# Half of a branch slab moved into a recurrent mixer's state scan, and gate products between its groups of small products

## The reference, cut to what matters

```python
# third branch: the recurrence, here in chunks of 64 positions
def step(state, inp):
    r_t, w_t, k_t, v_t, kk_t, a_t = inp
    sa = jnp.einsum("bhvk,bhk->bhv", state, kk_t)
    state = (state * w_t[:, :, None, :]
             - sa[..., None] * (kk_t * a_t)[:, :, None, :]
             + v_t[..., None] * k_t[:, :, None, :])
    return state, jnp.einsum("bhvk,bhk->bhv", state, r_t)
...
gates = jax.nn.sigmoid(proj[..., OFF_GATE:OFF_RWKV].reshape(b, s, N_BRANCH, D_MODEL) + gate_b)
branches = jnp.einsum("bsnc,ncd->bsnd", ys, branch_proj)   # ys: conv, attention, recurrence
merged = jnp.einsum("bsnd,bsnd->bsd", gates, branches)
return merged @ w_mix_out, v_first
```

## Time and profile before

| what | us |
|---|---|
| median of 3 runs | 1669.34 |
| lowest and highest run | 1667.26, 1671.3 |
| the profiled execution, in all | 1670.32 |
| its span, first to last instruction | 1667.9 |

### The profile page before, as it was taken

The page is one execution under the profiler, slowest core; times in us unless marked ns, Lnnn a source line. Parts: engine busy times, 40 slices in busy tenths (PEclk is TensorE's granted clock), DMA queues, the critical chain, the costliest instruction groups (busy, mean ns, idle before and its releaser), DMA issues.

```text
span 1667.9 us, 29552 instructions
## 1 busy us (share of the span) xinstructions
PE 1633.1 (98%) x12590; PEld 1497.5 (90%) x12590; DVE 1239.9 (74%) x1358; ACT 922.4 (55%) x1015; POOL 37.5 (2%) x40
## 2 busy tenths in 40 slices
PE   8999999999999999999999999999999999999997
PEld 7988998999999998888999988888888897988887
DVE  6677877975788888776697787657876678677655
ACT  5376534544566557554576655448555456555445
POOL 0000000100000000000020000000000000000000
PEclk9999999999999999999999999999999998999999
DMA  8524445453454544555633455553555541445551
GB/s 295 185 90 169 160 143 202 153 206 122 158 197 181 201 161 167 202 195 187 212 133 127 165 212 188 181 198 130 201 199 189 169 177 72 167 179 184 189 187 54
DMA packets 84136, 287.14 MB, mean 172 GB/s; under 512 B 5856, under 2 KB 54112, under 8 KB 56384
## 3 DMA queue, kind: packets, MB, share of 16 engines
q1 hardware_dynamic: 79984, 273.70, 46.6%
q0 software_dynamic: 2816, 10.69, 1.8%
q10 hardware_dynamic: 1232, 1.25, 0.2%
HBM read 281.42 MB, written 4.19 MB: 171 GB/s over the span
## 4 chain that ended last, share of the span: by engine, by line
PE 86%; DVE 7%; ACT 3%; issue 1%; DMA 1%; POOL 0%; ACTq 0%; DVEq 0%; POOLq 0%
PE PS L476 86%; DVE arena L2151 2%; DVE ring_lo L2148 2%; ACT arena L1484 1%; DVE arena L2148 1%; ACT ring_hi L1484 1%; DMA arena<-spilled_gates 1%; DMA residual<-in_x_t 0%; ACT L1484 0%; ACT operand L1484 0%; DVE arena L2308 0%; DMA ring_raw<-in_w_stream 0%; DVE inv L2207 0%; DVE residual L2148 0%; PE PS L922 0%
## 5 line engine op out<-in xcount | busy, mean ns | idle before, releaser
L476 PE MATMUL PS<-operand,ring_hi 128*128 128x256 f32 (+1 forms) x4360 | 905.6, 329 | 12.7 <-DVE operand L2213 10.2
L476 PEld LDWEIGHTS PS<-operand,ring_hi 128*128 128x128 f32 x4360 | 727.6, 191 | 80.3 <-DVE ring_lo L2148 8.1
L2148 DVE TENSOR_TENSOR ring_lo<-ring_raw,ring_hi 128x2048 fp32r<-128x2048 f32 (+2 forms) x267 | 601.8, 2257 | 203.6 <-ACT ring_hi L1484 203.1
L1484 ACT ACTIVATE ring_hi<-ring_raw 128x2048 fp32r<-128x2048 f32 (+2 forms) x267 | 497.2, 1863 | 192.3 <-PE PS L476 184.7
L476 PE MATMUL PS<-operand,ring_lo 128*128 128x256 f32 x3060 | 601.9, 283 | 0.1
L476 PEld LDWEIGHTS PS<-operand,ring_lo 128*128 128x128 f32 x3060 | 479.9, 192 | 12.0 <-DVE ring_lo L2148 0.4
L1484 ACT ACTIVATE arena<-PS 128x512 f32<-128x512 f32 (+2 forms) x141 | 89.7, 642 | 175.9 <-PE PS L476 164.0
L476 PE MATMUL PS<-hidden,ring_hi 128*128 128x512 f32 x704 | 174.8, 396 | 0.0
L476 PEld LDWEIGHTS PS<-hidden,ring_hi 128*128 128x128 f32 x704 | 128.0, 188 | 26.2
L2148 DVE TENSOR_TENSOR arena<-arena,PS 128x512 f32<-128x512 f32 (+4 forms) x147 | 99.6, 683 | 28.0 <-ACT arena L1484 21.6
L1484 ACT ACTIVATE arena<-arena 128x512 f32<-128x512 f32 (+6 forms) x124 | 85.4, 702 | 59.8 <-DVE arena L2151 32.8
(11 more groups left out here) (160 smaller groups left out, 1125.0 us busy)
## 6 DMA issues: line engine op xcount, KB each, us to landing
ring_raw<-in_w_stream SPq DMA_DIRECT2D x215, 1024.0 KB, 4.8
ring_raw<-in_w_stream SPq DMA_DIRECT2D x64, 512.0 KB, 4.4
ring_raw<-in_w_stream SPq DMA_DIRECT2D x52, 256.0 KB, 3.5
spilled_gates<-arena POOLq DMA_DIRECT2D x12, 256.0 KB, 2.7
arena<-spilled_gates POOLq DMA_DIRECT2D x2, 1536.0 KB, 9.8
tables<-in_tables POOLq DMA_DIRECT2D x1, 1344.0 KB, 9.7
residual<-in_x_t ACTq DMA_DIRECT2D x4, 256.0 KB, 7.7
arena<-in_mem_t POOLq DMA_DIRECT2D x1, 1024.0 KB, 16.6
```

What stands on the lines that cost most here:

```text
L476: return nc.tensor.matmul(out, lhs, rhs, start=start, stop=stop, skip_group_check=True)
L1484: return nc.scalar.activation(out, in_, func, **kw)
L2148: return v.tensor_tensor(out, a, b, op)
```

## The change

- gate_half takes a range of tiles, so that a half can be issued in two pieces.
- gate_slab(4), which stood ahead of the second pairs, is issued as one half ahead of them and one behind. On VectorE the masking of these pairs goes ahead of take_gates(4).
- In the levels, the first three tiles (9 MATMULs) of the second gate half stand between add_to_yt and add_to_y, the other five behind add_to_y.
- Output tiles 2 and 3 of branch slab 0 (24 of its 48 MATMULs, bank 7) are issued in the scan, in three pieces: 9 behind added and carrier, 9 ahead of propagated(2), 6 between carried(2) and carried(3). The waits for the operand and for the slab's low part move ahead of the first piece. Tiles 0 and 1 stay behind the scan.
- So that bank 7 is free, added(1) goes to the second half of bank 2, added(0) and added(2) to the halves of bank 6.
- ScalarE's copy of the transitions waits for the second rk_update in place of a signal of its own.
- VectorE's split of the slab gates + 14 (the third branch slab) goes behind rk_out.

The number of products and of instructions on VectorE and ScalarE stays as it is.

```diff
-            def gate_half(n, m):
+            def gate_half(n, m, ks=range(KT)):
...
-                for k in range(KT):
+                for k in ks:
                     last_ = block_product(out, slot, m * KT + k, XH[:, k, :], XL[:, k, :], k == 0, k == KT - 1)
-                if m == 1:
+                if m == 1 and k == KT - 1:
...
-            gate_slab(4)
+            gate_half(4, 0)
             pe.wait_ge(sem("rk_masked"), 1)
             token_pairs(4, K_, KK).then_inc(sem("rk_pairs"), 1)
+            gate_half(4, 1)
...
                     last.then_inc(sem("rk_dyt"), 1)
+                gate_half(5 + li, 1, range(0, 3))
                 for j in range(8):
...
                 last.then_inc(sem("rk_dy"), 1)
-                gate_half(5 + li, 1)
+                gate_half(5 + li, 1, range(3, KT))
...
-                o = bank(6 + c)[rows_of(q), tt * 4 * HD + f * HD:tt * 4 * HD + (f + 1) * HD]
+                first = (0, 4, 4)[gc] * HD + f * HD
+                o = bank(2 if c else 6)[rows_of(q), first:first + HD]
...
+            operands(2)
+            pe.wait_ge(lo_split, place(START["branch"])[2] + 1)
+
+            def branch_products(m, ks):
+
+                for k in ks:
+                    last_ = block_product(tiles_of(6, 4)[:, m, :], place(START["branch"])[0], 4 * m + k, XH[:, 8 + k],
+                                          XL[:, 8 + k], k == 0, k == 3)
+                return last_
...
-            low.then_inc(sem("rk_transition"), 1)
             up.then_inc(sem("rk_update"), 1)
+            branch_products(2, range(0, 3))
...
-            pe.wait_ge(sem("rk_transition"), 2)
+            pe.wait_ge(sem("rk_transition"), 1)
...
+            branch_products(2, (3,))
+            branch_products(3, range(0, 2))
             pe.wait_ge(sem("rk_state"), 2)
             propagated(2)
...
             carried(2).then_inc(sem("rk_carried"), 1)
+            branch_products(3, range(2, 4))
...
-            operands(2)
-            branch_slab(0, 6)
+            branch_products(0, range(4))
+            branch_products(1, range(4)).then_inc(multiplied, 1)
...
-            act.wait_ge(sem("rk_transition"), 1)
+            act.wait_ge(sem("rk_update"), 2)
...
-            take_gates(4)
             dve.wait_ge(sem("rk_pairs"), 2)
             masked_results(Fm, 4, "before", "rk_masked")
+            take_gates(4)
...
-                step(tt_(new, new, chunk_part(7) if gc == 1 else chunk_part(6, 1), ALU.add))
+                step(tt_(new, new, chunk_part(2 if gc == 1 else 6, 1), ALU.add))
...
             next_state(2)
-            split_slab(START["gates"] + 14)
             dve.wait_ge(sem("rk_inner_copied"), 1)
...
             last.then_inc(sem("rk_out"), 1)
+            split_slab(START["gates"] + 14)
             output_gains()
```

## The result

The changed kernel takes 1675.3 us (median of 7 runs, 1672.1 to 1676.7) against 1669.3: ratio 1.0032, 95% interval 1.0023 to 1.0041, so 5.3 us slower, outside the range of the prediction and above its bound for a change. The profiled execution took 1672.1 us, its span is 1670.1; it is the fastest of the seven, so its trace shows less of the loss than the median does.

What follows compares the result with a forecast made beforehand. Bound after the scan: VectorE's rk_out, the gates' reload, then VectorE's fixed chain to 307.57, not TensorE's end of slab 0. The terms put the gates 1.0 us later, so 1669.3 + 1.0 = 1670.3 us, range 1666.5 to 1673.0.

Steps and rivals of the forecast that it cites:

- The reload: Gates' reload after rk_out: the slab issued in its way costs between 0 and 2.7 us; gates land at 281.6, 1.0 later.
- TensorE's head start on slab 0: After the scan: TensorE some 1.45 us ahead on branch slab 0, then idle about 3 us before branch slab 4.
- the rule of turns between queues: In the reload: DMA engines alternate queues packet by packet, so the slab's whole 2.7 us is paid: 282.5, 1671.2 at the end.
- rival 1: Reload goes in order of request, memory operand off the path; only rk_out counts: -0.8, 1668.5 us; chance 0.20.
- rk_out: VectorE's signal behind the scan comes at 266.4, 0.8 us earlier; the scan's last small product ends at 265.4.
- Up to the scan: Gate slab 4 and the levels together: 0.3 + 1.4 - 1.44 - 0.7 = -0.45 us.
- The stalls near 188 and 200: TensorE's late instruction blocks at 189.38 and 200.35: the change wins 1.44 us at the first, 0.7 at the second.
- the cuts: In levels 1 to 4, a run of 128 small products is cut in two: 4 x 0.35 = 1.4 us lost.
- the gate slab's part: Gate slab 4 split round the second pairs: one more switch, +0.3 us; stall near 188 gone, -1.44.
- The levels' part: Nine gate products between Yt's and Y's groups: +1.4 us for cut runs, -0.7 for covering the stall at 200.35.
- Rival 3: Block behind gate slab 5 still late: 1.44 us not won, the second stall's 0.7 falls too; 1672.4 us; chance 0.15.
- rival 2: Scan stalls are waits that inserted products fill; VectorE's chain has slack: -2.3, 1667.0 us, at best 1664.0; chance 0.13.

Runs made afterwards that it cites:

- second profiles: One more execution of each kernel, unchanged: the kernel before, 1666.7 us, and the changed kernel, 1675.0 us.
- b1: The kernel before with only the split of slab gates + 14 moved behind rk_out: 1672.4 us, ratio 1.0019.
- b4: The kernel before with only the 24 branch products in the scan, with their banks and ScalarE's wait; split in its old place: 1673.5 us, ratio 1.0023.
- a3: The changed kernel with the split of slab gates + 14 back in its old place, ahead of the additions: 1673.9 us, ratio 1.0028 to the kernel before.
- a1: The changed kernel with SP holding the load of weight slab branch + 5 until the gates have landed: 1669.3 us, 1.0000 of the kernel before.
- c1: The kernel before with the split of slab gates + 14 behind rk_out and the load it releases held until the gates have landed: 1669.2 us, ratio 0.9992.
- d0: The changed kernel once more, unchanged, for a second profile: 1675.0 us, one execution.

## Why the prediction was wrong

The forecast was 1670.3 with no change that can be measured; it is 1675.3. The step that failed is the price of the slab in the reload's way, taken at 1.8 us and measured at 3.8 to 4.2. The frame held: the chain over rk_out, the reload and VectorE's fixed 27 us is what sets the end, and TensorE's head start on slab 0 was spent on standing still (3.3 us of idleness before slab 4, predicted about 3). Three terms in the frame were off, all to the same side, the reload's by the most.

**The reload (+1.8 taken, +3.8 in the shown pair, +4.2 by the second profiles).** The prediction had both ends, 0 and 2.7, and took a value between them. The slab's issue came at 269.97, 2.5 us behind rk_out as predicted (268.9 said, for an rk_out 1 us earlier than it came). In the window 274 to 278 of the changed kernel the two queues moved, side by side,

```profile
q1 hardware_dynamic: 135, 1.00, 62.3%
q0 software_dynamic: 157, 0.58, 36.4%
```

so for four microseconds the gates (q0) got little more than a third of the engines. In the same window before, q0 had all of it:

```profile
q0 software_dynamic: 367, 1.44, 97.9%
```

62% of all engines over 4 us is 2.5 us, and a slab is 143 packets, of which 8 fall outside the window: about the full 2.7 us. The two queues move 135 and 157 packets, nearly one for one, and those of the slab are twice as large. This is the rule of turns between queues of the Trainium skill ("DMA: Bandwidth & Descriptors", Queues, rings and completion order), and here the trace agrees with it; the prediction quoted it, had its number (282.5) and didn't take it. What it gave as the trace's agreement, a later transfer that starts when the slab ends, was no evidence for turns: the block of the earlier trace rows that waits for the slab speaks rather for its rival 1. The turns stood in another row of the window of the earlier trace rows, where a transfer of POOL's moves beside the slab:

```profile
q0 software_dynamic: 130, 0.46, 27.7%
```

By the rule alone the time would have been 1671.2. The cause of the further 1.1 to 1.6 us in the changed kernel isn't shown. The nearest is the second slab, issued at 278.56: its bytes take two thirds of the engines while the last gates are under way (VectorE goes on at 284.73; window 282.5 to 286):

```profile
q1 hardware_dynamic: 111, 0.91, 67.8%
q0 software_dynamic: 116, 0.47, 34.3%
```

Against it as the whole cause stands b1, whose slabs are issued at the same distances from POOL's issue and share the engines in the same way, and which has 2.6 and not 3.8. No run takes the second slab away by itself.

**rk_out (-0.8 predicted, +0.3 measured; from slab 11 on -0.35 and +0.6).** The scan was to end at 265.4 and ends at 266.6 (265.90 + 0.68). The nine products ahead of the inner group filled VectorE's 1.21 us as predicted, but they end just where a block of instructions ends, and the next one wasn't there: 0.74 us (from 256.02 to the second stall the trace has 127 products, with their loads one more block). The second stall grew from 1.3 to 1.59. My sum had treated the blocks' arrival as fixed in time and 0.45 us earlier; TensorE went on at 259.92, 0.7 later than before and 1.2 later than in the sum. b4 shows the direction of this part alone (26.3 to POOL in place of 25.2), a3 how far it can go (28.2, with the same program from slab 11 on). The 2.2 us that the moved split was to save are in it, as a1 (25.7) and a3 (28.2) show: without them rk_out would have been 3 us late.

**Up to the scan (-0.45 predicted; -0.1 against the shown profile, +2.0 against the second one).** This is the step that I would teach. The stalls near 188 and 200, 2.15 us, were read from one profile and entered as certain gains. The price of the cuts was right: 4 x 0.35 = 1.4, and 1.6 measured, with 0.2 at 240.20, where TensorE now waits for VectorE's last Y. But the gains exist in some executions only. Where the first stall comes (four of six traces) it costs 2.8 us on the mean, the fall of the clock included, so the gate slab's part is 0.67 x 2.8 - 0.4 = 1.5 us of gain, and 1.5 (0.2 to 3.0) was measured. That the two agree so well is luck with six traces. The levels' part won nothing in any run. The second stall stands in one trace of fourteen, behind the first; that it is a consequence of the first one's lateness is argued, and b4 and c1 have the first without it.

Added up over a typical pair: the cuts 1.6, the gate slab -1.5, rk_out 0.6, the reload 3.8 to 4.2: 4.5 to 4.9 us, against 5.3 measured.

By the medians of the runs the parts agree less well. In three pairs the medians lie further apart than the marks: 2.9 against 1.3 us in b1, 4.1 against 1.1 in b4 (both by the kernel before), 6.0 against 3.9 to 4.5 between a1 and the changed kernel. The mean granted clock goes the same way: over all runs it was 0.9939 in the changed kernel, 0.9935 in a3 and b4, 0.9949 to 0.9954 in the kernel before and 0.9961 in a1. So some of the loss may be clock in executions that no trace shows; no run tests it.

**The rivals.** Rival 3 was to end on the slow side, by the block behind gate slab 5 still being late. Its result (slower by about 3) is the nearest, its mechanism is refuted: in none of the eight traces with the new order is the block late; it moved at 181.7 in the changed kernel, where 181.9 was predicted. Rival 1 is refuted by b1, rival 2 by the stall of 1.59 us that stays in the scan while branch products run on both sides of it.

**What was to show it.** Right: no gap at 188 and 200, runs of 64, one gap over 1 us in the scan, TensorE's 3 us before slab 4. Wrong: POOL's issue (267.0 said, 268.04), VectorE's idleness ahead of the gates (3 to 4 said, 5.2).

## What to carry to other kernels

When a wait or a piece of work is moved, follow the transfer that its signal releases to the queue, and ask what is on the DMA engines at that moment; a megabyte that was free ahead of the reload cost 2.6 to 4.2 us when it was issued 4.8 us later, and one wait on the issuing queue gave it back. Filling an idle TensorE is worth nothing where the chain has already left it for VectorE and a transfer. And a stall that has no wait behind it in the code is to be looked for in a second execution before it is entered as a gain.

## What the runs showed of the hardware that I had not expected

The supply of TensorE's instructions is a race of well under a microsecond against the weight stream. The same program had its block moved at 183.7 (no stall) in one execution and behind the slab, in 187 to 188.3 (1.2 us idle, and 0.5 more 12 us later), in another; the slab's bytes had begun 0.6 us later in the first, counted from gate slab 4. The Trainium skill ("Runtime: NRT & Kernel Launch", Instruction fetch mechanics) has fetch mostly hidden and room for 2048 instructions on TensorE; the trace disagrees: each block moved only some 1.2 us after TensorE had entered the one before, and the stalls come at distances of 256 and 512 instructions, 1.3 us long after runs of a few hundred small products.

A stall can cost more than its own length. Behind 2.15 us (b4) and 1.80 us (c1) of idleness the granted clock went to 0.50 for about three microseconds, and the stretch from slab 4 to slab 11 lost 1.7 us more than the stall itself, where it lost 0.3 to 0.4 more behind the shorter ones. The length alone doesn't decide it: in d0 it fell behind a stand of 1.94 us, and behind the 3.29 us before branch slab 4 in the changed kernel's first profile it didn't fall. In d0 the fall cost nothing, as TensorE only had less to wait for there.

The granted clock also differs between executions: its mean was 0.997 in the changed kernel's profile and in a1's, 0.994 in b1's, 0.995 in the one of before. From the last wait of the stage to the end, where all kernels are the same, the span took between 1358.4 and 1360.4 us. For differences of a few microseconds the marks inside a trace say more than the times of the whole.
